# The first stage of a two-block transformer kernel: adaptive vectors in halves of 512 columns, first linear weight by weight

## The reference, cut to what matters

```python
cond = silu(c)                                   # c: (1, 1024)
mod = cond @ w_ada[0] + b_ada[0]                 # 6 vectors of 1024
sh1, sc1, gt1, sh2, sc2, gt2 = split(mod, 6)     # numbered 0..5 below
h = rmsnorm(x, g_mix[0]) * (1 + sc1) + sh1       # x: (512, 1024)
cq = rmsnorm(h @ w_dq, g_q)                      # 1024 -> 384
q = cq @ w_uq                                    # 384 -> 8 heads x (128 + 64)
ckv_kr = h @ w_dkv                               # 1024 -> 256 + 64
kv = rmsnorm(ckv_kr[:256], g_kv) @ w_ukv         # 256 -> 8 heads x (128 + 128)
```

## Time and profile before

| | before |
|---|---|
| median of 3 runs | 2257.37 us (2255.49 to 2258.55) |
| profiled execution | 2252.95 us |
| its span | 2250.9 us |
| granted TensorE clock, mean | 0.992 |
| PE / DVE / ACT / POOL busy | 2181.1 / 1418.2 / 965.0 / 184.9 us |

### The profile page before, as it was taken

The page is one execution under the profiler, slowest core; times in us unless marked ns, Lnnn a source line. Parts: engine busy times, 40 slices in busy tenths (PEclk is TensorE's granted clock), DMA queues, the critical chain, the costliest instruction groups (busy, mean ns, idle before and its releaser), DMA issues.

```text
span 2250.9 us, 31890 instructions
## 1 busy us (share of the span) xinstructions
PE 2181.1 (97%) x13239; PEld 1927.5 (86%) x13239; DVE 1418.2 (63%) x2129; ACT 965.0 (43%) x1460; POOL 184.9 (8%) x159
## 2 busy tenths in 40 slices
PE   6999999999999999999999999999999999999999
PEld 3877988888898898898898999997778889899998
DVE  5777565656577667565556667754665545666674
ACT  3556442213256645453443434434444334443443
POOL 7310000000032100000020000002012001000001
PEclk8999999999999999999999999999999999999999
DMA  6542245555521122332421332323112332233231
GB/s 237 162 145 90 89 169 187 187 189 185 187 83 57 39 66 85 113 99 90 132 75 62 113 105 96 109 89 111 52 47 80 122 105 64 66 122 106 88 108 56
DMA packets 128325, 245.70 MB, mean 109 GB/s; under 512 B 4843, under 2 KB 36934, under 8 KB 128054
## 3 DMA queue, kind: packets, MB, share of 16 engines
q1 hardware_dynamic: 123424, 228.02, 30.3%
q0 software_dynamic: 4096, 15.28, 2.1%
q10 hardware_dynamic: 662, 0.37, 0.1%
HBM read 241.56 MB, written 2.10 MB: 108 GB/s over the span
## 4 chain that ended last, share of the span: by engine, by line
PE 83%; DVE 9%; ACT 3%; DMA 2%; issue 2%; POOL 0%; SPq 0%; DVEq 0%; ACTq 0%
PE PS L66 82%; DVE t L75 5%; ACT t L72 3%; DVE t L83 2%; DVE t L86 1%; DMA t<-in_ffn_w_dram 1%; PE PS L69 1%; DMA t<-in_w_ada_dram 1%; DVE t L79 1%; DMA t<-in_w_ff_dram 0%; DVE t L92 0%; DVE t L80 0%; POOL t L75 0%; SPq L101 0%; DVE PS L75 0%
## 5 line engine op out<-in xcount | busy, mean ns | idle before, releaser
L66 PE MATMUL PS<-t,t 128*128 128x256 f32 (+4 forms) x12872 | 2134.1, 328 | 38.8 <-DMA t<-in_w_ada_dram 8.7
L66 PEld LDWEIGHTS PS<-t,t 128*128 128x128 f32 (+2 forms) x12872 | 1884.0, 188 | 285.0 <-issue 50.4
L72 ACT ACTIVATE t<-t 128x1024 fp32r<-128x1024 f32 (+7 forms) x738 | 654.3, 903 | 935.2 <-DVE t L75 462.1
L75 DVE TENSOR_TENSOR t<-t,t 128x1024 fp32r<-128x1024 f32 (+9 forms) x693 | 778.2, 1139 | 377.6 <-ACT t L72 330.6
L72 ACT ACTIVATE t<-PS 128x512 f32<-128x512 f32 (+4 forms) x327 | 174.9, 549 | 216.8 <-PE PS L66 166.1
L75 POOL TENSOR_TENSOR t<-t,t 128x512 f32<-128x512 f32 (+2 forms) x71 | 86.2, 1215 | 1091.2 <-ACT t L72 932.9
L75 DVE TENSOR_TENSOR t<-t,PS 128x512 f32<-128x512 f32 (+2 forms) x134 | 83.1, 625 | 145.5 <-PE PS L66 139.2
L72 ACT ACTIVATE t<-t,t 128x256 fp32r<-128x256 f32 (+5 forms) x220 | 115.8, 535 | 95.7 <-DVE t L83 44.8
L83 DVE SCALAR_TENSOR_TENSOR t<-t,t,t 128x1024 f32<-128x1024 f32 (+2 forms) x157 | 144.4, 926 | 16.7 <-DMA t<-in_w_ada_dram 11.0
L83 DVE SCALAR_TENSOR_TENSOR t<-PS,t,t 128x512 f32<-128x512 f32 (+3 forms) x128 | 82.1, 648 | 87.8 <-PE PS L66 82.2
L75 DVE TENSOR_TENSOR t<-t 128x512 f32<-128x512 f32 (+4 forms) x104 | 74.2, 714 | 16.2 <-ACT t L72 15.8
(11 more groups left out here) (30 smaller groups left out, 166.9 us busy)
## 6 DMA issues: line engine op xcount, KB each, us to landing
t<-in_w_ff_dram SPq DMA_DIRECT2D x64, 1024.0 KB, 5.2
t<-in_ffn_w_dram SPq DMA_DIRECT2D x60, 1024.0 KB, 5.1
t<-in_w_ada_dram SPq DMA_DIRECT2D x36, 1024.0 KB, 6.4
t<-in_w_ada_dram POOLq DMA_DIRECT2D x24, 512.0 KB, 4.5
t<-in_w_in_dram SPq DMA_DIRECT2D x12, 1024.0 KB, 5.1
t<-in_swa_w_qkv_dram SPq DMA_DIRECT2D x6, 1024.0 KB, 5.7
t<-in_ffn_w_dram SPq DMA_DIRECT2D x8, 768.0 KB, 4.4
t<-in_w_in_dram SPq DMA_DIRECT2D x24, 256.0 KB, 3.6
```

The source lines that it names most:

```text
L66: return Instr(self.real and self.real.matmul(o, lhs, rhs, start=start, stop=stop, **more))
L72: return Instr(self.real and self.real.activation(o, src, func, **more))
L75: return Instr(self.real and self.real.tensor_tensor(o, a, b, op))
```

## The change

- Vectors 0 and 1 are summed together by DVE: a tile holds, for 128 rows of w_ada, columns 512 ch to 512 ch + 511 of both vectors (16 tiles of 512 KB, ch 0 or 1, k 0 to 7). ch 0 gives shift and gain of feature chunks 0 to 3, ch 1 those of 4 to 7. `pe_row` and the two mods go; each half gets eight one-column products.
- SP loads x in four pieces, then ch 0, with dq's first weight between, then ch 1, with the second; none of these loads waits.
- The norm's squares are taken on x as it lies (tokens on partitions) by DVE; ACT scales x by the inverse root before a second set of transposes, so no R is needed. h is made in place in HN0 from that.
- dq runs weight by weight: both token halves through the first weight (chunks 0 to 3), then both through the second.
- ACT issues the loads of `invf` and positions first; POOL no longer adds squares, so its angles begin when those are there, with two side tiles issued between SIN and COS, once weight 0's low part is written.
- Side tiles: two fewer in `dve_mla_in` before dkv ends, one fewer in each of the next two places, three more behind maxima 4, 5, 6. Columns of vector 2 move from before ukv to between its weights, those of vector 4 from behind uq 2 to behind uq 3.

```diff
+        FIRST_PARTS = {0: [(0, k) for k in range(6)], 1: [(0, 6), (0, 7)] + [(1, k) for k in range(4)],
+                       2: [(1, k) for k in range(4, 8)]}
+        def dve_first(e, ch, ks):
+            for k in ks:
+                buf, tile, c = ACC2[ch][:, :, :], FIRST_TILES[ch, k][:, :, :], SILUC[:, k:k + 1]
+                e.wait_ge(landed_first[ch, k], (ch, k))
...
+                    e.scalar_tensor_tensor(buf, tile, c, buf, ALU.mult, ALU.add).then_inc(ada_acc, (0, ch, k))
+        def pe_first_columns(e, ch):
...
+            e.wait_ge(ada_acc, (0, ch, 7))
...
         def pe_begin(e):
...
-            pe_row(e, 4, 0, 0, 0)
-            pe_row(e, 5, 0, 0, 1)
-            e.wait_ge(misc, "ones")
-            pe_sums(e, "n0", 0, lasthf=F, add=ssq_pool)
-            pe_sums(e, "n0", 1, lasthf=F, add=ssq_pool)
-            pe_mod(e, 0, 1)
-            pe_row(e, 6, 0, 0, 2)
-            pe_row(e, 7, 0, 0, 3)
...
+            pe_x_scaled(e, ALL)
+            b = banks.take("warm", (acc, "warm"))
+            e.wait_for(banks.free("warm"))
+            e.wait_ge(landed_first[0, 5], (0, 5))
+            for _ in range(4):
+                t = e.matmul(PS[:, b, :], ones, X[:, 0, :], start=True, stop=True)
+            t.then_inc(acc, "warm")
+            pe_first_columns(e, 0)
         def act_begin(e):
...
+            e.activation(RS[:, 0:4], RS[:, 0:4], ACT.Sqrt, bias=EPSC, scale=1.0 / D).then_inc(root, "n0")
+            e.wait_ge(recip, "n0")
+            for t4 in range(4):
+                e.activation(XSC[:, t4, :], XIN[:, t4, :], ACT.Copy, scale=RS[:, t4:t4 + 1]).then_inc(x_gain, t4)
             for j in range(8):
                 e.wait_ge(acc, ("x", j))
                 e.activation(X[:, j, :], PS[:, banks["x", j], :], ACT.Copy).then_inc(x_init, j)
-                e.wait_ge(x_init, j)
-                act_square(e, "n0", j, F, X[:, j, :], add=ssq_pool)
...
+            for j in range(8):
+                if j == 6:
+                    act_split(e, 0)
+                e.wait_ge(acc, ("xs", j))
+                e.activation(HN0[:, j, :], PS[:, banks["xs", j], :], ACT.Copy).then_inc(x_turned, j)
+            act_first_hi(e, 0, LOWER)
+            act_first_h(e, LOWER, COLS[1])
+            act_first_hi(e, 1, LOWER)
             act_split(e, 1)
-            act_normed(e, n0, 1, ALL)
+            act_first_h(e, UPPER, COLS[F])
+            act_first_hi(e, 0, UPPER)
+            act_first_hi(e, 1, UPPER)
         def dve_begin(e):
...
+            dve_x_squares(e, range(4))
...
+            e.wait_ge(root, "n0")
+            e.reciprocal(RS[:, 0:4], RS[:, 0:4]).then_inc(recip, "n0")
+            dve_first(e, 0, range(4))
             e.wait_ge(acc, "columns")
...
+            dve_first(e, 0, range(4, 6))
+            dve_at["vec"] = (0, 0)
             dve_split(e, 0)
...
+            dve_first(e, 0, range(6, 8))
+            dve_first_columns(e, 0)
+            dve_first_h(e, LOWER)
+            dve_lowered(e, 0, LOWER)
+            dve_first(e, 1, range(3))
+            dve_lowered(e, 1, LOWER)
+            dve_first(e, 1, range(3, 5))
             dve_split(e, 1)
-            dve_normed(e, n0, 1, ALL)
+            dve_first(e, 1, range(5, 8))
+            dve_first_columns(e, 1)
+            dve_lowered(e, 0, UPPER)
+            dve_lowered(e, 1, UPPER)
...
+        def pe_dq(e):
...
+            for u, w in enumerate(WX["dq"]):
+                if u:
+                    pe_first_columns(e, 1)
+                pe_step(e, w)
+                for hf in range(2):
+                    for n, (c, wd) in enumerate(THREE):
...
-            pe_columns(e, 0, 2)
             for hb, w in enumerate(WX["ukv"]):
+                if hb:
+                    pe_columns(e, 0, 2)
                 pe_step(e, w)
...
             pe_uq(e, 2)
-            pe_columns(e, 0, 4)
             pe_m_turn(e, 0)
...
             pe_uq(e, 3)
+            pe_columns(e, 0, 4)
             pe_m_scores(e, 4)
...
             dve_m_max(e, 4)
-            dve_beside(e)
+            dve_beside(e, 2)
             dve_m_max(e, 5)
             dve_m_soft(e, 3)
-            dve_beside(e)
+            dve_beside(e, 2)
             dve_m_max(e, 6)
-            dve_beside(e)
+            dve_beside(e, 2)
             dve_m_soft(e, 4)
             dve_m_max(e, 7)
             dve_beside(e)
```

More of the change, by code:

```diff
@@ L977, in act_vectors @@
                     e.dma_start(V1[r:r + k, :], A_[name]).then_inc(vec_in, by=16)
[L978 to L994, removed]
+            e.dma_start(V2[:, :], A["b_ada"].rearrange("l (j p) -> (l j) p", p=128)).then_inc(vec_in, "all", by=16)
@@ new lines, in pe_first_columns @@
+        def pe_first_columns(e, ch):
+            b = banks.take(("mod", 0, ch), (mod, (0, "sum", ch)))
+            e.wait_for(banks.free(("mod", 0, ch)))
+            e.wait_ge(ada_acc, (0, ch, 7))
+            e.wait_ge(misc, "ones")
+            for v in range(2):
+                for j in range(4):
+                    t = e.matmul(PS[:, b, 4 * v + j:4 * v + j + 1], ACC2[ch][:, v, 128 * j:128 * j + 128], ones[:, 0:1],
+                                 start=True, stop=True)
+            t.then_inc(acc, ("mod", 0, ch), ("mod", 0, 0, ch))
@@ new lines, in pe_begin, with pe_x_scaled @@
+            b = banks.take("warm", (acc, "warm"))
[5 more added lines that the diff above has]
+            pe_first_columns(e, 0)
+        def pe_x_scaled(e, chunks):
+            for j in chunks:
+                b = banks.take(("xs", j), (x_turned, j))
+                e.wait_for(banks.free(("xs", j)))
+                for t4 in range(4):
+                    e.wait_ge(x_gain, t4)
+                    t = e.transpose(PS[:, b, t4 * 128:(t4 + 1) * 128], XSC[:, t4, j * 128:(j + 1) * 128], ident)
+                t.then_inc(acc, ("xs", j))
@@ new lines, in act_first_h, with act_first_hi @@
+        def act_first_h(e, chunks, cs):
+            for j in chunks:
+                e.wait_ge(x_turned, j)
+                e.wait_ge(mod, (0, "gain", j // 4))
+                e.activation(HN0[:, j, cs], HN0[:, j, cs], ACT.Identity, bias=MOD[:, 0, j:j + 1],
+                             scale=GS[:, 0, j:j + 1]).then_inc(x_gain, ("h", j, 1))
+        def act_first_hi(e, hf, chunks):
+            for j in chunks:
+                cs = COLS[hf]
+                if hf == 0 and j in LOWER:
+                    e.wait_ge(hmul, ("n0", j, 0))
+                else:
+                    e.wait_ge(x_gain, ("h", j, 1))
+                e.activation(HHI[:, j, cs], HN0[:, j, cs], ACT.Copy).then_inc(h_hi, ("n0", j, hf))
@@ L1056, in act_begin, with dve_first_h @@
+            act_first_hi(e, 0, UPPER)
+            act_first_hi(e, 1, UPPER)
+            ta.hand([(acc, ("mod", 0, 0, 1))], 0, 1)
             ta.only(0, 1, 2, 4)
+        def dve_first_h(e, chunks):
+            e.wait_ge(mod, (0, "gain", 0))
+            for j in chunks:
+                e.wait_ge(x_turned, j)
+                e.tensor_scalar(HN0[:, j, 0:256], HN0[:, j, 0:256], GS[:, 0, j:j + 1], MOD[:, 0, j:j + 1], ALU.mult,
+                                ALU.add).then_inc(hmul, ("n0", j, 0))
@@ new lines, in dve_lowered, with dve_x_squares @@
+        def dve_lowered(e, hf, chunks):
+            cs = COLS[hf]
+            for j in chunks:
+                e.wait_ge(h_hi, ("n0", j, hf))
+                e.tensor_tensor(HLO[:, j, cs], HN0[:, j, cs], HHI[:, j, cs].bitcast(F32), ALU.subtract).then_inc(
+                    h_lo, ("n0", j, hf))
+        def dve_x_squares(e, t4s):
+            for t4 in t4s:
+                e.wait_ge(x_in[t4], "x")
+                if t4 > 1:
+                    e.wait_ge(x_sq, t4 - 2)
+                e.tensor_tensor_reduce(out=JUNK[t4 % 2][:, :], in0=XIN[:, t4, :], in1=XIN[:, t4, :], scale=1.0, scalar=0.0,
+                                       op0=ALU.mult, op1=ALU.add, accum_out=RS[:, t4:t4 + 1]).then_inc(x_sq, t4)
@@ L1094, in pool_begin @@
         def pool_begin(e):
-            for j in range(1, 7):
-                add_square(e, "n0", j, F, add=ssq_pool)
             step = [0]
@@ L1109, in pool_begin @@
             for dst, quarter in ((SIN, 0.0), (COS, 0.25)):
+                if dst is COS:
+                    pool_beside(e, 2)
                 ts(PA[:, :], PB[:, :], 1.0 / TWO_PI, quarter, ALU.mult, ALU.add)
```

146 lines of the change are left out of this document (89 added, 57 removed).

## The result

| | before | after |
|---|---|---|
| median of 20 runs each, taken together, us | 2256.48 | 2259.88 |
| profiled execution, us (span) | 2252.95 (2250.9) | 2261.05 (2259.2) |
| mean granted clock of the profiled execution | 0.992 | 0.988 |

What follows compares the result with a forecast made beforehand. TensorE's matmuls were taken to bound the kernel (busy 2181.1 of 2250.9 us). Terms -3.5, +1.85, +0.4 and +0.5 sum to -0.75; 2252.2 plus 4.42 gives 2256.6 us, range 2253 to 2261, with two rivals 2250 to 2264.

Steps and rivals of the forecast that it cites:

- First stage: Everything up to dq's end: dq starts at 34.8 instead of 49.27 and ends at 68.8 against 72.3, -3.5 us.
- The gain of the first half: First stage, first vector half: its gain is ready at 33.1 us, after sums and one-column products.
- VectorE beside POOL's cosine round: Second half's VectorE queue, 15.9 us alone, is lengthened 3.1 us by three POOL additions and some wide steps.
- The columns of the second half: PE's one-column products before dq's second weight: they take 2.0 us, ending at 54.1.
- Later stages: Everything behind dq: moved columns, a longer pause and late side tiles together cost 1.85 + 0.4 + 0.5 us.
- (a): Columns of vector 2 between ukv's weights: formerly free inside a PE wait, now costing +1.85 us, low end 0.
- The longer pause, +0.4: Before ukv's second weight, PE's pause of 3.6 instead of 1.74 us lets the clock fall earlier: +0.4, bounds 0 to 1.
- (b): Vector 4's columns behind uq 3: turn 0 loses its 2.45 us bank wait, maximum 2 starts 3.1 to 3.4 earlier.
- (c): Three more side tiles behind maxima 4, 5, 6: 4.0 us on VectorE, partly taken up by waits; +0.5 with (b).
- The port: Rival: POOL's one-tensor operations also take turns with VectorE in the second half, 5.4 plus 2 us, 2264.0; chance 0.12.
- The softmaxes at their full price: Rival: the late side tiles in the softmax stage cost 4.0 us instead of 0.5, 2260.1; chance 0.10.
- The engines miss each other: Rival: angle additions hardly meet VectorE's sums (-3.1, -1.0) and the clock is up again (-2.5), 2250.0; chance 0.22.

Runs made afterwards that it cites:

- a2: The kernel after, with before's places for layer 0's side tiles and columns: 2257.95 us, ratio 1.0003.
- a5: The kernel after, with before's places for side tiles and columns, and vector 4's columns in bank 7: 2253.14 us, ratio 0.9988.
- a6: The kernel after, with POOL's rotation of the second half's query rows back ahead of two side tiles' issues: 2258.61 us, ratio 1.0012.
- b2: The kernel before, with only vector 4's columns put in bank 7: 2252.74 us, ratio 0.9988.
- b1: The kernel before, with after's places for side tiles and columns, first stage untouched: 2260.27 us, ratio 1.0020.
- a1: The kernel after, with POOL's cosine round waiting for the last sum of the second half: 2255.37 us, ratio 0.9991.
- a3: The kernel after, with five unused 512-column products on PE ahead of the second half's columns and four behind: 2257.40 us, ratio 1.0002.
- a7: The kernel after, first half's last low parts behind its last two sums, ScalarE making rows and high parts in turns: 2256.54 us, ratio 1.0000.
- c2: c1 with POOL issuing the third and fourth side tile in the middle of its cosine round: 2239.70 us, ratio 0.9924.
- c1: The kernel after with edits of a1, a5, a7, eight filler products around the second half's columns and two side tiles summed behind its gain: 2249.12 us, ratio 0.9970.

## Why the prediction was wrong

**First stage: I said -3.5, and by the runs it was nothing (+0.7, -1.4 and 0.0 in three pairs).** In the marks I had dq's end at 68.8; it came at 75.0 to 75.5 in a2, a5 and a6 and at 76.63 in after. I also started from a quick execution: 72.31 for before, where b2 and b1 have 73.65 and 74.49. The 7.8 us between 68.8 and 76.63, along the chain as I had laid it:
- *The gain of the first half: 35.3 instead of 33.1, 2.2* (34.3 to 34.7 in a1, a2, a5 and a6). The reciprocal came at 14.47 (13.3), because the last two squares took 1.62 and 1.65, where the first two took 1.22 and 1.27; POOL worked beside all four, so why the last were longer is not shown. The first columns took 2.86 in after and 1.9 to 2.1 in a2, a5 and a6.
- *VectorE beside POOL's cosine round, the step whose mechanism failed: 4.7 instead of 3.1.* The additions were nearly right, 3.0 for the 3 x 0.87 = 2.6. The one-tensor steps were not: I gave them 0.5, for two wide steps, and they cost 1.7, most of it on small instructions, the four h rows (0.6) and single low parts (0.82 instead of 0.42 beside them). I had priced small low parts in the rival (2 us there), by the one of the earlier trace rows with 1.25, and not in the forecast. The uncontended queue was 16.2 for my 15.9, another 0.3. a1 shows the whole term by itself, the traces its parts.
- *The columns of the second half: 3.54 instead of 2.0.* I had the clock low for the weight (2.5, which a3 gives as 2.7) and forgot it for the products that stand in the same pause. a3 shows this too. (The 55.9 that I read from the earlier trace rows as the end of the low clock is 55.7.)
- *ScalarE's four rows: 2.9 instead of 2.3,* by the timeline of ACT. The rest, 1.4, is the second weight, 12.5 instead of 11.1: at the full clock it took 9.8 (a3), where I had 8.6.

a7 shows that the order of the first stage's queues, which I took as given, was worth about as much as any of these, 3.2.

**Later stages: I said +2.75; a2 gives 2.5 and b1 4.5.** They make all of the measured 3.4. The parts hold less well than the sum. (a) Columns between ukv's weights, +1.85, stood (1.8). "The longer pause, +0.4" was named for the wrong thing: the low stretch behind it was 3.4 us long in before and in after alike. What the pause did was to grow by 1.1 more through POOL's rotation, a move that I had passed over: the change has it, and I counted only POOL's DMA issues there. (b) Turn 0 without its bank: -3.1 to -3.4 said, -3.4 at maximum 2 in b2. (c) The late tiles: with (b) taken off, +3.75 said and 3.5 found, as what is left over. The waits that I let "take up part" took up little.

**The rivals.** *The port* has the right direction and a wrong size: of its 7.4 us on top of my 3.1, 1.6 came. The Trainium skill ("SBUF — State Buffer", Who interferes with whom) says that a VectorE instruction with two SBUF inputs contends with any GpSimd instruction that reads SBUF. Here it is POOL that waits when its step has one tensor and VectorE's is wide: the sum at 43.20 took 1.45 where 1.27 is its own time, the one at 47.43 took 1.27, and POOL's step beside the first took 2.35, where such a step took 1.49 with VectorE idle (32.41 in after). Beside an addition the sum at 40.99 took 2.11. So the trace agrees that they contend, and which of the two engines waits set the price. *The softmaxes at their full price* came out at 2260.1, next to the measured 2259.88. That is luck: it kept the -3.5 of the first stage, which did not come, and set the later stages at +6.25. *The engines miss each other* did not come; a1's wait makes them miss.

**The time.** I carried the 4.42 us between the profiled execution and the median over as a constant, and it was not one: 3.5 for before with all 20 runs, -1.2 for after. This is why the marks of the profiled pair say +8.3 and the medians +3.4.

Of the signs that I named, the hole in PE, the low clock, turn 0's bank and the two side steps between the maxima were right. The first dq product was to come near 35 and came at 37.7, VectorE was to stand idle some 4 us before the first weight's low part and did for 1.84, and "wrong if dq ends after 72" came true with 76.6.

## What to carry over

When work moves beside another engine, price every step of the neighbour against whatever it can meet, its one-tensor steps and your small instructions too: here three additions cost 3.0 us whichever instructions met them, and the steps that I had nearly left out 1.7. Where an engine's pause holds a few products, they can run at the low clock too, and so can what follows; filling the pause with products on data at hand was worth 2.7 us here. Look at which bank, which queue and which DMA issue an early step stands behind: one argument (bank 7) gave 2.7 us, and one DMA issue moved up gave 9.4. And don't size a part of a change by one pair of traces: kernels with the same first stage stood 2.2 us apart at its end. Make the same edit on several kernels and compare the runs.

## What the runs showed of the hardware

**The same short pause is followed by the low clock in one execution and not in another.** A pause of PE of 0.87 us, ended by VectorE, stands at 1158.64 us in before and at 1165.31 in after. Windows of PE behind it, before and then after:

```profile
1168.00:1171.00 3.00, 3.00 (x25) 1.00 0.60 177
```

```profile
1168.00:1171.00 3.00, 3.00 (x21) 0.73 0.03 5
1171.00:1174.00 3.00, 3.00 (x21) 0.70 0.00 0
```

In after the clock fell behind it and stayed at half for 3.4 us, in a5 for 6.8, in before and c2 not at all; before and c2 have a second pause there instead, of 1.15 us, which the slower PE of after and a5 does not have. Between the last turn and the last product, the low stretches add up to 6.8 us in before and in c2, 13.7 in a5, 17.1 in after and in b1, and 20.5 in a7. From the last turn to the end of the span it is 2041.4 in after and 2039.0 in before, 2.4 of the 8.3 between the two spans, with the same products in both. How much of it is the clock is open: b1, with as much of it low as after, took 2039.9. What decides where the clock falls is not shown here either: it was seen in single executions.

**The lower level lasts well beyond a wait.** It held for 6.1 us of products behind the 4.33 us wait at 64.17, and for 6.7 behind 5.08 us in c1. The Trainium skill ("TensorE: Matmul & The Clock Gate", HAM oscillation — how this bites in real kernels) has TensorE fall to its slow clock during waits for DMA and start the next piece cold. That agrees; the trace adds that in after it is VectorE's and ScalarE's queues that make such a wait, with no DMA in it. In c1 a late side tile is behind it.
